# A weight ring of five chunks, eleven gather slots, and attention kind by kind, in a streaming encoder layer with PEER experts

## The reference, cut to what matters

```
n    = RMSNorm(x)
proj = n @ w_in        # fox q|k|v|forget | sb q|k|v | gate_fox | gate_sb, 5120 columns and 8
y_fox = softmax(q.k/8 + C[t] - C[s]) v      over s <= t   (C: running sum of log forget)
y_sb  = stick-breaking(q.k/8) v             over s <  t   (a reverse running sum over keys)
h    = x + (sig(gate_fox)*(y_fox@w_o_fox) + sig(gate_sb)*(y_sb@w_o_sb)) @ w_out
q    = RMSNorm(h) @ w_peer_q                # 8 heads x 2 halves x 128
pick the top 16 of 128 keys per half, the top 16 of the 256 sums per head
out  = h + sum over 8*16 picks of gate * gelu(expert_u[e] . n2) * expert_v[e]
```

## Time and profile before

| | us |
|---|---|
| median of 3 runs | 4281.25 (4277.36 to 4287.47) |
| the profiled execution | 4279.13 |
| its span, first to last instruction | 4277.3 |
| PE busy | 3242.6 (76%) |
| DVE busy | 2864.9 (67%) |
| ACT busy | 1216.8 (28%) |
| POOL busy | 1389.5 (32%) |
| mean granted clock of PE | 0.823 |
| moved by DMA | 1388 MB, 325 GB/s over the span |

### The profile page before, as it was taken

The page is one execution under the profiler, slowest core; times in us unless marked ns, Lnnn a source line. Parts: engine busy times, 40 slices in busy tenths (PEclk is TensorE's granted clock), DMA queues, the critical chain, the costliest instruction groups (busy, mean ns, idle before and its releaser), DMA issues.

```text
span 4277.3 us, 32195 instructions
## 1 busy us (share of the span) xinstructions
PE 3242.6 (76%) x9738; PEld 1679.2 (39%) x9738; DVE 2864.9 (67%) x5568; ACT 1216.8 (28%) x2591; POOL 1389.5 (32%) x1086
## 2 busy tenths in 40 slices
PE   8989838588868595798876785899876677868665
PEld 3345623244435242455453332555453233334222
DVE  2012477587678975688579775788679766557865
ACT  1132112255311121566111121666211245111110
POOL 0000013243433333343333232334333233434553
PEclk9966969687879798788888897888888777888787
DMA  4413439899999889799999798787998788999997
GB/s 138 134 53 120 141 139 415 335 380 400 391 370 386 322 328 414 279 383 374 390 392 360 278 400 345 298 348 307 384 391 328 277 316 324 408 420 385 385 420 321
DMA packets 306602, 1388.17 MB, mean 325 GB/s; under 512 B 36384, under 2 KB 96960, under 8 KB 159968
## 3 DMA queue, kind: packets, MB, share of 16 engines
q0 software_dynamic: 154464, 1116.02, 64.7%
q1 hardware_dynamic: 121056, 243.75, 15.9%
q10 hardware_dynamic: 30912, 26.35, 1.9%
HBM read 1350.49 MB, written 35.10 MB: 324 GB/s over the span
## 4 chain that ended last, share of the span: by engine, by line
PE 35%; DVE 28%; DMA 18%; ACT 7%; issue 6%; SPq 5%; POOL 1%; ACTq 0%; DVEq 0%; POOLq 0%
DVE uv L1346 11%; PE pb L946 9%; DMA uv<-expert_uv,rows_u 8%; PE pv L777 7%; SPq L526 5%; DMA arena<-w_main 5%; PE pb L887 3%; PE pb L860 3%; PE pb L730 3%; PE pb L759 2%; PE pb L835 2%; DVE held L1369 2%; DMA arena<-w_stream 2%; PE pv L946 2%; DVE arena L1407 1%
## 5 line engine op out<-in xcount | busy, mean ns | idle before, releaser
L680 POOL DMA_INDIRECT uv<-expert_uv,rows_u x1024 | 1334.8, 1304 | 2250.8 <-PE pv L777 1168.8
L777 PE MATMUL pv<-uv,diag 128*128 128x512 f32 x2316 | 1244.7, 694 | 377.4 <-ACT diag L1083 336.9
L1346 DVE CUSTOM_DVE_ANT_0 uv<-uv,nr 128x1024 f32<-128x1024 f32 x1056 | 1241.5, 1220 | 204.8 <-DMA uv<-expert_uv,rows_u 171.0
L777 PEld LDWEIGHTS pv<-uv,diag 128*128 128x128 f32 x2316 | 504.0, 226 | 1024.7 <-issue 982.4
L946 PE MATMUL pb<-arena 128*128 128x512 f32 x1280 | 620.9, 643 | 163.2 <-DMA arena<-w_main 163.1
L1369 DVE SCALAR_TENSOR_TENSOR held<-uv,wgt,held 128x1024 f32<-128x1024 f32 x477 | 613.0, 1285 | 16.9 <-DVE wgt L1357 0.3
L1090 ACT ACTIVATE gel<-dots 128x4 f32<-128x4 f32 x264 | 54.2, 205 | 1792.2 <-DVE dots L1346 1712.5
L946 PEld LDWEIGHTS pb<-arena 128*128 128x128 f32 x1280 | 258.9, 207 | 497.0 <-issue 316.9
L730 PE MATMUL pb<-arena 64*128 64x512 f32 (+6 forms) x544 | 281.2, 635 | 125.2 <-DVE arena L1328 43.0
L759 PE MATMUL pb<-arena 128*128 128x64 f32 (+3 forms) x1728 | 256.2, 297 | 40.3 <-ACT o L1072 40.3
L759 PEld LDWEIGHTS pb<-arena 128*128 128x128 f32 (+3 forms) x1728 | 237.1, 202 | 106.6 <-issue 68.5
(11 more groups left out here) (147 smaller groups left out, 2670.5 us busy)
## 6 DMA issues: line engine op xcount, KB each, us to landing
arena<-w_main SPq DMA_DIRECT2D x80, 1024.0 KB
arena<-w_stream SPq DMA_DIRECT2D x80, 1024.0 KB
uv<-expert_uv,rows_u POOLq DMA_INDIRECT x1024
arena<-x SPq DMA_DIRECT2D x16, 512.0 KB, 19.6
scratch_gates<-arena ACTq DMA_DIRECT2D x32, 256.0 KB, 11.3
arena<-scratch_gates SPq DMA_DIRECT2D x8, 1024.0 KB, 21.7
arena<-scratch_c_p SPq DMA_DIRECT2D x8, 520.0 KB
arena<-x_t SPq DMA_DIRECT2D x8, 512.0 KB
```

What stands on the lines that cost most here:

```text
L680: pool.indirect_dma_start(out=uv[k % NU][:].rearrange("p a n -> p (a n)"), out_offset=None, in_=io["expert_uv"][:, :], in_offset=bass.Indi ...
L777: mm = nc.tensor.matmul(pv[:, c * BANK:(c + 1) * BANK], diag[n % ND][:], uv[k % NU][:, 1, c * BANK:(c + 1) * BANK], start=n == first, stop ...
L1346: nc.vector.tensor_tensor_reduce(out=u, in0=u, in1=row[:], scale=1.0, scalar=0.0, op0=ALU.mult, op1=ALU.add, accum_out=dots[b % 2][:, k % ...
```

## The change

It makes the ring `wring` five chunks long and the gather ring eleven slots. The room (the arena shrinks from 22640 to 20568 numbers per partition) comes from four things. The attention's units are ordered kind by kind within a pair of heads: four FoX units, then four SB units; a "pair" in the plan is now one kind of a pair of heads, and a set of buffers holds one kind. There are two sets for the prompt tiles, three for the samples, which get a layout of their own. The buffers for the running sums go from three to two. The probabilities share one ring of four over both kinds. In the merge, the x rows lie on the attention's output rows, the norm row and the small buffers of the choosing lie on the gates. So SP waits for the outputs to be turned before it loads the x rows, and for the merged rows before it loads the norm row.

```diff
-NU = 10
+NU = 11
-NW = 3
+NW = 5
-ARENA = 22640
+ARENA = 20568
@@ Plan
                 for hp in range(PAIRS):
-                    for hh in range(2):
-                        for t in sub:
-                            ti = sum(subs, ()).index(t)
-                            for k in range(KINDS):
+                    for k in range(KINDS):
+                        for hh in range(2):
+                            for t in sub:
+                                ti = sum(subs, ()).index(t)
                                 self.units.append((g, len(self.pairs), len(self.cks), hp, hh, t, ti, t - sub[0], k))
-                        self.cks.append((g, sub, hp * 2 + hh))
-                    self.pairs.append((g, sub, hp))
+                            if k == 0:
+                                self.cks.append((g, sub, hp * 2 + hh))
+                        self.pairs.append((g, sub, hp, k))
...
+        for i, (g, sub, hp, k) in enumerate(self.pairs):
+            b = (i - self.first_pair[g]) % (3 if sub[0] == SAMPLES else 2)
+            total[b] += 16 * (6 if sub[0] == SAMPLES else 4)
+            self.pair_set.append(b)
+            self.pair_loaded.append(total[b])
@@ stream
-        o = [[sb(f"o{k}{i}", [P, WID]) for i in range(2)] for k in range(KINDS)]
+        o_rows = [sb(f"o{i}", [P, KINDS, WID]) for i in range(2)]
+        o = [[o_rows[i][:, k, :] for i in range(2)] for k in range(KINDS)]
+        xh = [o_rows[i][:].rearrange("p k n -> p (k n)") for i in range(2)]
...
+        at[0] = ARENA - (KS + 10 * PW + 2 * P)
+        kt0, vt0, qt0 = carve(KS), carve(10, PW), carve(2 * P)
         at[0] = 0
+        rooms = [AttentionRoom([kt0, carve(KS)], [vt0, carve(10, PW)], [qt0, carve(2 * P)], [carve(KS) for _ in range(2)],
+                               [carve(KS) for _ in range(4)], [carve(KS) for _ in range(2)], [carve(10, P) for _ in range(2)])]
...
+        g_row = gate[1][:, 1, :]
@@ load_pair
-                    if i >= 2:
-                        sp.wait_ge(summed_up, plan.pair_last[i - 2] + 1)
+                    sets = 3 if sub[0] == SAMPLES else 2
+                    if i >= sets:
+                        sp.wait_ge(summed_up, plan.pair_last[i - sets] + 1)
...
@@ load_ck
-                    if i >= 3:
-                        sp.wait_ge(minimum, plan.kind_no[plan.ck_last[i - 3]] + 1)
+                    if i >= 2:
+                        sp.wait_ge(minimum, plan.kind_no[plan.ck_last[i - 2]] + 1)
@@ SP, attention
                                 load_pair(i)
-                            load_ck(2 * i)
-                            load_ck(2 * i + 1)
+                            if pair[3] == 0:
+                                load_ck(i)
+                                load_ck(i + 1)
@@ SP, merge
+                    sp.wait_ge(o_turned, tiles[-1] + 1)
                     for ti, t in enumerate(tiles):
                         r = query_rows(t)
                         sp.dma_start(xh[ti][0:r], io["x"][first_row(t):first_row(t) + r, :]).then_inc(x_in[ti], 16)
-                    sp.dma_start(g_row, io["norm_ffn"].partition_broadcast(P)).then_inc(g_in, 16)
                     for c in range(NW, 8 + NW):
+                        if c == NW + 4:
+                            sp.wait_ge(merged, 2 * (tiles[-1] + 1))
+                            sp.dma_start(g_row, io["norm_ffn"].partition_broadcast(P)).then_inc(g_in, 16)
                         load_chunk(g, c)
@@ PE, ACT and DVE: one ring of four for the probabilities
-                    if i >= 2:
-                        before = plan.unit_of[1, i - 2]
-                        act.wait_ge(turned, plan.turns[before][-1][0] + 1)
+                    if n >= 4:
+                        act.wait_ge(turned, plan.turns[n - 4][-1][0] + 1)
-                    z, mag = prob[1][i % 2], low[i % 2]
+                    z, mag = room(t).prob[n % 4], room(t).low[i % 2]
```

More of the change, by code:

```diff
@@ L12 @@
 from contextlib import ExitStack
+from dataclasses import dataclass
 import concourse.bass as bass
@@ L124 @@
              "samples": 1}
+@dataclass
+class AttentionRoom:
+    kt: list
+    vt: list
+    qt: list
+    ck: list
+    prob: list
+    low: list
+    probt: list
 class Projections:
@@ L309, in stream @@
         sel = sb("sel", [P, NS])
-        stat = sb("stat", [P, 2, 4])
+        stat = sb("stat", [P, 4, 4])
         st = sb("st", [P, 4])
@@ L353, in stream @@
         mt = carve(KD, 2 * P)
[L354 to L358, removed]
         top = [carve(2, HEADS, TOPK) for _ in range(2)]
@@ L362, in stream @@
         sc, ex, ci = carve(HEADS, TOPK), carve(HEADS, TOPK), carve(HEADS, TOPK).bitcast(U32)
+        g_row = gate[1][:, 1, :]
+        rest = [gate[0][:, 0, i * BANK:(i + 1) * BANK].rearrange("p (j n) -> p j n", j=4) for i in range(2)]
+        qh = [gate[0][:, 1, i * BANK:(i + 1) * BANK].rearrange("p (a q) -> p a q", a=2) for i in range(2)]
+        n2t = ot
+        hit = gate[0].rearrange("p k (h n) -> p (k h) n", h=HEADS // 2).rearrange("p h (a b) -> p h a b", a=TOPK)
+        cand = gate[1].rearrange("p k (h n) -> p (k h) n", h=HEADS // 2)
+        rest2 = mt
+        at[0] = gates_at + KINDS * D
         cab, caf = carve(2, HEADS, TOPK).bitcast(U32), carve(2, HEADS, TOPK)
@@ L371, in stream @@
         sq = carve(BANK)
-        tst_more = [carve(BANK) for _ in range(2)]
+        tst = [carve(BANK) for _ in range(2)]
         ss, rstd = carve(ABREAST), carve(ABREAST)
@@ L413, in stream @@
         sk_in = sem("sk_in")
-        pair_in = [sem(f"pair_in{i}") for i in range(2)]
-        ck_in = [sem(f"ck_in{i}") for i in range(3)]
+        pair_in = [sem(f"pair_in{i}") for i in range(3)]
+        ck_in = [sem(f"ck_in{i}") for i in range(2)]
         scored = sem("scored")
@@ new lines, in load_pair @@
+                    if sub[0] != SAMPLES:
+                        w = keys_of(sub[-1])
+                        here(qt[b][:, 0:n * P], q[rows, META + t0 * P:META + (t0 + n) * P])
+                        here(kt[b][:, 0:w], key[rows, 0:w])
+                        here(vt[b][:, 0:t0 + n, :], v_p[META:w, rows].rearrange("(j p) n -> p j n", p=P))
+                        here(vt[b][0:META, 8, :], v_p[0:META, rows])
+                    else:
+                        here(qt[b][:, 0:NS], q[rows, NP:T])
+                        here(kt[b][:, 0:PAST], key_past[rows, :])
+                        here(kt[b][:, PAST:KS], key[rows, NP:T])
+                        here(vt[b][:, 0:8, :], v_past[META:PAST, rows].rearrange("(j p) n -> p j n", p=P))
+                        here(vt[b][0:META, 8, :], v_past[0:META, rows])
+                        here(vt[b][0:NS, 9, :], v_s[:, rows])
@@ L722, in scores @@
                     diag_at = w - r
-                    half = slice(hh * DH, (hh + 1) * DH)
-                    pe.wait_ge(pair_in[pair % 2], plan.pair_loaded[pair])
+                    half, b = slice(hh * DH, (hh + 1) * DH), plan.pair_set[pair]
+                    pe.wait_ge(pair_in[b], plan.pair_loaded[pair])
                     for m, c0, c1 in plan.pieces[n]:
@@ L729, in scores @@
                         masked = c1 > diag_at
-                        mm = nc.tensor.matmul(pb[0:r, m % 3, 0:c1 - c0], qt[k][pair % 2][half, tj * P:tj * P + r],
-                                              kt[k][pair % 2][half, c0:c1], start=True, stop=not masked)
+                        mm = nc.tensor.matmul(pb[0:r, m % 3, 0:c1 - c0], room(t).qt[b][half, tj * P:tj * P + r],
+                                              room(t).kt[b][half, c0:c1], start=True, stop=not masked)
                         if masked:
@@ L1052, in turn_out @@
                     r = query_rows(plan.units[n][5])
+                    probt = room(plan.units[n][5]).probt
                     if n >= 2:
```

98 lines of the change are left out of this document (36 added, 62 removed).

## The result

The changed kernel takes 4301.8 us (median of 20 runs, 4278.9 to 4326.8) against 4282.1 (20 runs, 4273.4 to 4293.2): a ratio of 1.0046, with a 95% interval of 1.0031 to 1.0061. It is slower by 20 us where I forecast 4220. Its runs also scatter more, over 48 us for 20.

The account below looks back on a forecast made before the run. Gathering stages were taken as transfer-bound except at joints, wave 3's attention as paced by DVE's order. Gains of 15, 45, 12, 6, 25 less 28, 8, 4 give 63 us: 4220 stated, range 4150 to 4300.

Parts of the forecast that it names:

- the slot: Eleventh gather slot: one more gather carried into each of seven transfer-bound stages, 12 us taken, bounds 0 and 17.
- term 4: Merge: chunks 3 and 4 no longer wait for gates, x rows and norm row; +6 us, bounds -15 and +22.
- term 2: Projection's end: chunk 19 no longer behind the first pair's loads, PE's 23.3 us wait goes; 15 us a wave, 45.
- term 1: Before the projections of waves 1 to 3: two more weight chunks loaded while the DMA idles, 15 us, bounds 0 to 15.
- Next late there: the forget sums, 4.1 us: Joint after the projection: the wait expected next once chunk 19's goes, 4.1 us in the chain, as before.
- Term 6: Attention, waves 1 to 3: shorter lead of a pair's load; stalls of 5, 5 and 2 us, 28 us charged.
- Term 5: Wave 4's attention: three sets of half size bring loads earlier, cutting PE's V-row waits; +25 us, bounds 0 and 43.
- Term 7: Attention units ordered kind by kind: light and heavy steps grouped, mostly smoothed by PE's lead; -8 us, bounds +10 and -30.
- Term 8: Wave 0, no gathers: earlier start +3 us, possible stalls at six pairs -7; -4 us, bounds +5 and -15.
- Rival (b): Attention's pair load becomes the bound, at 24 to 27 us with stalls at 18 pairs: about 4332 us; chance 0.17.
- the signs of being right: Projections: no 23 us w_main wait, joint DMA share over 0.85; wave 4: no out_sv_s wait over 5 us.
- wrong altogether: Wave 3's attention over 40 us longer than 382, or projections of waves 1 and 2 no shorter than 224 and 237.

Follow-up runs that it names:

- runs 6 and 4: Three weight chunks for five: in the changed kernel with a third prompt set 4250.9 us, in the changed kernel itself 4354.2 us.
- run 7: Changed kernel with a third prompt set, three weight chunks, and each wave's first pair loaded at column 8, behind half 19: 4225.3 us.
- run 8: Changed kernel with a third prompt set and four weight chunks for five: 4196.3 us, against 4202.5 with five.
- run 5: Kernel before, with the loads of a wave's first pair issued at column 8, behind half 19, instead of column 7: 4271.0 us, ratio 0.9970.
- run 9: Changed kernel with a third prompt set and five chunks, ten gather slots for eleven: 4220.2 us, ratio 0.9860.
- run 3: Changed kernel, two prompt sets, V's bytes loaded from long rows of the turned keys instead of 512-byte rows (attention values wrong): 4187.0 us, ratio 0.9781.
- run 1: Changed kernel with a third set of buffers for the prompt tiles, samples' sets unchanged: 4202.5 us, ratio 0.9805 to the kernel before.
- run 2: Kernel before, with only the order of units changed to four FoX, then four SB, and one probability ring: 4278.1 us, ratio 0.9991.
- run 11: Changed kernel with three prompt sets, and four sets instead of three for the samples' wave: 4145.0 us, ratio 0.9689.
- run 10: Changed kernel with a third prompt set, running sums loaded without waiting for the gate columns' stores: 4195.5 us, ratio 0.9799.

## Why the prediction was wrong

**Terms 1 to 4, the joints: the right sign, too small, and partly for other reasons.** I had 15 + 45 + 12 + 6 = 78 us from preloaded chunks, chunk 19, the slot and the merge. The stretches between attentions gave 100, and 5 more behind wave 4. Nearly all of it lies in the projections: from SyncE's first `w_main` chunk to the first running sums it is 308 us for 274 after the change in wave 1, 380 for 350 in wave 2 and 383 for 350 in wave 3. From the first `w_stream` chunk to there a wave became at most 2 us shorter, so term 4 had 6 us that hardly came. What a stage wins is not what the kernel wins: with three chunks for five the projections are 79 and 84 us longer (runs 6 and 4), the whole kernel 48 and 52. Half 19's place is some 26 of that (run 7), where term 2 had 45, and the rest comes with the depth; whether the fifth chunk gives its half of term 1's 15 these runs can't tell (run 8). "Next late there: the forget sums, 4.1 us" was the weak sentence: that wait became 74 us in all (run 5 shows it arise). The slot is worth about 18 us (run 9) for the 12 taken and the 17 of the full count.

**Term 6, the failed step.** The lead was right on average in waves 2 and 3, 11.2 and 13.7 us for the 12 and 13 predicted, and 8.2 for 11 in wave 1. The load was mis-sized. I had its price from both sides, 4 and 27 us, and took 18, 17 and 13 "nearer to" wave 4's half pair of 19. Measured, one kind took 22.5, 22.3 and 20.6 us where PE waited on it. Halving a pair's time was the error: in wave 4 itself one kind took 19 to 35 us in the changed kernel, where half of the whole pair had been 19. It was not a quiet road that made that row short, for the DMA engines were full while the pair landed:

```profile
3471.66:3509.84 38.18, 15.38 (x70) 7.36 (x68) 23.47 (x35) 16.26 (x35) 9.88 (x9) 0.75 0.97 372
```

Why the whole pair went quicker than two kinds do stays open (2912 rows by the code in 38.2 us are 0.21 us a row on its engine, below the 0.28 of run 3). The other row, SyncE's 54 us for the eight loads of wave 2, with its half of 27, was nearer, but not clean either: PE waited for weight chunks until 1654.7, 1674.0 and 1685.9 us, so weights landed in that time too, and "33 GB/s of 415" counts too few bytes.

The other part of the miss is what a stall costs. I had stalls of 5, 5 and 2 us at six pairs a wave, 72 us, and charged 28 of them, since "PE runs a step ahead of DVE". The waits were 130 us, and the attentions of waves 1 to 3 grew by 118, of which the third set gives 107 back (run 1). PE's lead hides little, since what a stall costs is not PE's time: while PE stands it frees no gather slot, the slots fill, and the DMA engines idle behind the stall (0.06).

**Term 5 failed by the same step.** Three sets of half the size have the lead of one step that two whole ones had, and one kind took more than half of the pair's time. Wave 4 gained nothing (285 for 282 us), where I had 25. PE's waits for V there went from 29.7 us in 2 times to 49 in 4. Four sets give what I had promised, and more (run 11): once the lead is long enough, the stage runs at a DMA share of 0.94.

**Term 7** had 8 us for the order: nothing (run 2). **Term 8** had 4 us lost in wave 0, and 3 were won.

**The rivals.** Rival (b) happened: the full-DMA price, from a load of about 20 us on. It had 4332 us against the 4302 measured. Beside it the joints and the end gave 27 us more, the stalls cost 118 where it had 144, terms 7 and 8 cost nothing where it had 12, and against that wave 4 did not give its 25. I gave it 0.17, though rows 6 spoke for it. The argument against it was that a stall fills the gather slots in 27 us and then frees the engines. The slots do fill, sooner, by the end of a stall of 12.5 us; but the engines come free only about when the load has landed, and that idle time is the loss. The sum as it should have stood: 4282 - 105 (joints, end) - 3 (wave 0) + 118 + 3 (wave 4 and its merge) = 4295; the median is 4302, and these stages are those of a quicker execution.

Of the signs of being right, two came: no 23 us wait for `w_main` at a projection's end (the longest is 11.1), and a DMA share over 0.85 at the joint of wave 2.

```profile
1680.00:1700.00 20.00, 3.84 (x7) 1.89 (x8) 8.13 (x10) 1.49 (x2) 4.83 (x4) 0.50 1.02 420
1700.00:1720.00 20.00, 16.02 (x40) 7.52 (x38) 18.19 (x31) 9.64 (x18) 4.80 (x4) 0.57 0.93 355
```

The third did not: wave 4 has waits for V rows of up to 17.2 us. The waits of L757 for V rows in waves 1 to 3, 13 recorded with a mean of 10 us, are nearer to the 12 that I had put down for (b) than to 2 to 5. Attention of wave 3 grew by 46 us; I had called over 40 wrong altogether.

## What to carry to other kernels

Halving what a buffer holds can cost far more than half of the time that its load has (here five steps became one): count the steps between the free and the first use again. Do not price half a load by halving the time of the whole; count its rows and what shares the DMA engines with them. Beside large packets a load's time went by its number of rows here, about 0.28 us for each on its engine, and more lead (a third set) or fewer, longer rows cured it. Then ask what a stall stops: here it held gather slots, and the DMA engines stood idle behind it. A wait taken away at a joint shows what was late next; look for that before the whole wait is booked as gain.

## What the runs showed of the hardware that I had not expected

The same bytes into the same buffers took 115 us less in 128 long rows than in up to 1024 rows of 512 bytes (run 3), though V is only some 15 of the 1388 MB moved (28672 rows of 512 bytes by the code). Two loads were used only 16.7 us behind their issue beside the gathers (run 10); without gathers ten loads had landed within 7.5.

The granted clock of PE falls with the stalls (its two levels are 1.2 and 2.4 GHz, and a row's figure is the mean of its stretch): 0.82 in the attention of wave 2 before, 0.79 with them, 0.82 again with three sets; in wave 4 0.75 with waits and 0.81 without. And the matmuls behind a stall are slower for it. The same six scores matmuls in wave 4 of the changed kernel, behind a stall and one unit later, with the stretches that give their clock:

```profile
3515.27 3.78 PE L757 MATMUL pb<-arena 64*32 64x512 f32 x6 [12.34 <-DMA arena<-out_fv_s]
3528.67 1.99 PE L757 MATMUL pb<-arena 64*32 64x512 f32 x6
```

```profile
3515.27:3519.00 3.73, 3.73 (x7) 0.89 (x7) 0.81 (x2) 0.00 (x0) 0.00 (x0) 0.50 0.49 185
3528.60:3530.60 2.00, 2.00 (x9) 0.60 (x8) 0.00 (x0) 1.81 (x6) 0.39 (x1) 1.00 1.00 401
```

They take 3.78 us at 0.50 and 1.99 at 1.00, and 3.78 behind each of the four waits for V rows in that wave. Yet PE's busy time in the stage is 202.9 us with the waits (run 1) and 202.4 without (run 11), since other units of run 11 run at the lower level (3.78 us too, behind idle times of 7.2 and 2.8 us in which PE waited for ACT). So a stall has a second price, 1.8 us for the scores behind it alone, though taking the waits away does not lower the stage's busy time.
